# Final normalisation inside the expert steps, one ranked tile per pair of steps, and weight pieces issued as soon as their buffer is free

## What is computed

```python
def trunk_layer(...):                      # 2048 prompt rows and 32 sample rows, 1024 wide
    m = hybrid_mixer(x, ...)               # convolution mixer and recurrent block
    x = layer_norm(ALPHA * x + m, ln1_g, ln1_b)
    x = layer_norm(ALPHA * x + hier_moe(x, ...), ln2_g, ln2_b)

def hier_moe(x, ...):                      # top-1 group of 4, then top-2 experts of its 4
    ...
    h = silu(xt @ moe_w1[e]) * (xt @ moe_w3[e])
    h = h * gates
    y = sum over the token's two experts of h @ moe_w2[e]
```

## Time and profile before

| | |
|---|---|
| median of 3 runs | 1303.81 us (1301.26 to 1305.11) |
| profiled execution, its own time | 1298.67 us |
| its span | 1296.6 us |
| PE busy | 1140.4 us, 88% |
| DVE busy | 782.8 us, 60% |
| ACT busy | 503.3 us, 39% |
| POOL busy | 153.0 us, 12% |
| DMA read from and written to HBM | 133.99 MB, 72.93 MB |

### The profile page before, as it was taken

The page is one execution under the profiler, slowest core; times in us unless marked ns, Lnnn a source line. Parts: engine busy times, 40 slices in busy tenths (PEclk is TensorE's granted clock), DMA queues, the critical chain, the costliest instruction groups (busy, mean ns, idle before and its releaser), DMA issues. The chain is left out here.

```text
span 1296.6 us, 20522 instructions
## 1 busy us (share of the span) xinstructions
PE 1140.4 (88%) x5818; PEld 1028.6 (79%) x5819; DVE 782.8 (60%) x1476; ACT 503.3 (39%) x650; POOL 153.0 (12%) x192
## 2 busy tenths in 40 slices
PE   6999999999999999999999757999999999996000
PEld 6999999999999997888887655888888888875000
DVE  5666554644564565665665664566666666632898
ACT  4554443633543453222222224455555554421000
POOL 1000000000000010023322250000000000000720
PEclk9999999999999999999999877999999999998555
DMA  5432565275430055154433166667667776522972
GB/s 182 134 93 67 131 130 104 82 145 105 78 105 20 21 158 170 66 163 163 162 131 84 67 188 239 201 252 276 231 240 278 280 250 221 198 99 92 407 287 101
DMA packets 82772, 207.39 MB, mean 160 GB/s; under 512 B 18064, under 2 KB 44720, under 8 KB 76464
## 3 DMA queue, kind: packets, MB, share of 16 engines
q0 software_dynamic: 21984, 100.53, 21.7%
q1 hardware_dynamic: 53840, 89.63, 20.6%
q10 hardware_dynamic: 6912, 16.79, 7.5%
HBM read 133.99 MB, written 72.93 MB: 160 GB/s over the span
## 5 line engine op out<-in xcount | busy, mean ns | idle before, releaser
L1227 PE MATMUL ps_h<-w_hi,xt_hi 128*128 x336 | 136.4, 406 | 0.0
L1227 PE MATMUL ps_h<-w_lo,xt_hi 128*128 x336 | 132.4, 394 | 0.0
L1227 PE MATMUL ps_h<-w_hi,xt_lo 128*128 x336 | 132.3, 394 | 0.0
L277 PE MATMUL ps_vb_c<-x_hi,w_hi 128*128 (+1 forms) x320 | 113.9, 356 | 11.2 <-DVE x_lo L441 11.2
L277 PE MATMUL ps_vb_c<-x_hi,w_lo 128*128 (+1 forms) x320 | 113.3, 354 | 0.0
L277 PE MATMUL ps_va_b<-x_hi,w_lo 128*128 (+1 forms) x320 | 112.7, 352 | 0.0
L277 PE MATMUL ps_vb_c<-x_lo,w_hi 128*128 (+1 forms) x320 | 112.6, 352 | 0.0
L277 PE MATMUL ps_va_b<-x_hi,w_hi 128*128 (+1 forms) x320 | 112.6, 352 | 0.0
L277 PE MATMUL ps_va_b<-x_lo,w_hi 128*128 (+1 forms) x320 | 111.8, 349 | 0.0
L1321 DVE TENSOR_TENSOR w_lo_p<-ps_o,w_hi_p 128x512 f32<-128x512 f32 x84 | 54.0, 685 | 54.4 <-PE ps_o L1211 54.4
L1018 DVE TENSOR_TENSOR w_lo<-w_raw,w_hi 128x2048 f32 (+1 forms) x32 | 73.1, 2287 | 11.8 <-ACT w_hi L1013 11.8
(11 more groups left out here) (260 smaller groups left out, 2580.6 us busy)
## 6 DMA issues: line engine op xcount, KB each, us to landing
w_raw<-in_w POOLq DMA_DIRECT2D x48, 1024.0 KB, 6.0
w_lo_p<-xs_scr SPq DMA_DIRECT2D x43, 512.0 KB, 4.7
o_scr<-w_lo_p SPq DMA_DIRECT2D x42, 512.0 KB, 2.7
w_raw<-in_w_in POOLq DMA_DIRECT2D x19, 512.0 KB, 3.6
x_raw<-in_x_t SPq DMA_DIRECT2D x20, 416.0 KB, 3.4
xs_scr<-x_raw ACTq DMA_DIRECT2D x16, 512.0 KB, 7.0
o_scr<-x_raw ACTq DMA_DIRECT2D x16, 512.0 KB, 8.4
x_hi_p<-y_scr SPq DMA_DIRECT2D x16, 512.0 KB, 4.5
```

Of the source, the lines that this page charges most:

```text
L277: mm = pe.matmul(ps[i][:, 0:CHUNK], w[:, i, k], x[:, k, bass.ds(c * CHUNK, CHUNK)], start=(k == 0 and n == 0), stop=(k == KT - 1 and n == 2))
L1227: mm = pe.matmul(ps_h[par][:], x[:, par, k], w[:, bass.ds(at, 1), k].rearrange("p o n -> p (o n)"), start=(k == 0 and n == 0), stop=(k == ...
```

## The change

**Order of tiles.** The output tiles are no longer in token order. DVE ranks the tokens by the later of their two experts (`later_experts`, `ranks`, with two counting matmuls on PE), so that a tile of 128 consecutive ranks is complete as soon as that expert has been stored. Tile 0 has 32 tokens, tiles 1 to 16 have 128. Records (token number, two slots) go to DRAM by 17 indirect writes of POOL in step 0 and come back by one load. Results are written to `y_out` by indirect DMAs.

**Place of the work.** `steps` unrolls four steps, loops over pair numbers 2 to 15 with the body skipped from `pairs - FTAIL` on (FTAIL = 13), and then runs 13 pairs that carry output tiles: with 21 pairs the first gather is in step 17, tiles 0 to 9 are summed in the even steps 18, 20, ... 36 and normalised in the odd steps behind them, and steps 38 to 41 each sum a tile (10 to 13) and, from 39, normalise the one before. What is left of tiles 13 to 16 follows the last step. The number of pairs is raised if a tile would not be complete in time. `v` has two buffers, `v1` one: `fetch` of a tile waits until the tile ahead has been summed, until the tile two ahead has landed in `y_out`, and until the steps that it reads have been stored.

**ACT** takes the root in the steps, and in all but the last step runs a small Silu behind it. **Weights**: POOL takes them in the step where the raw buffers are freed (a flag in the plan), two experts ahead, without the waits for the landing of the piece ahead. **Zeros**: `fill` writes five blocks of `o_scr` each time, where it wrote two.

```diff
+FLAST = 2
+FPAIR = NT - 3 - 2 * FLAST
+FTAIL = FPAIR + FLAST + 1
+OFILL, STORED = 5, 8
+PLAN = 2 * ((STEPS - NT) // 2 + 1 + FTAIL)
...
-                for rows in (xs_scr[bass.ds((q * 2 + i) * CAP, P), :], o_scr[bass.ds((q * 2 + i) * P + (STEPS - NE) * P, P), :]):
-                    act.dma_start(rows, zero).then_inc(s_zo, 16)
+                act.dma_start(xs_scr[bass.ds((q * 2 + i) * CAP, P), :], zero).then_inc(s_zo, 16)
...
+            for i in range(OFILL):
+                act.dma_start(o_scr[bass.ds((q * OFILL + i + STORED) * P, P), :], zero).then_inc(s_zo, 16)
...
+            for s in range(4):
+                emit(s, s % 2, s // 2, 2, None)
+            eng.wait_ge(s_pairs, 1)
+            pairs = eng.value_load(planned[0:1, 0:1], min_val=0, max_val=PLAN // 2 - FTAIL - 2) + (FTAIL + 2)
+            with eng.Fori(2, PLAN // 2 - FTAIL) as h:
+                with eng.If(h < pairs - FTAIL):
+                    emit(h * 2, 0, h, 2, None)
+                    emit(h * 2 + 1, 1, h, 2, None)
...
+            def pair(f, b, h):
+                emit(h * 2, 0, h, 2, (None, (f, b), None))
+                emit(h * 2 + 1, 1, h, 2, ((f + 1, 1 - b), None, (f, b)))
+
+            h = pairs - FTAIL
+            emit(h * 2, 0, h, 2, None)
+            emit(h * 2 + 1, 1, h, 2, ((0, 0), None, None))
+            for f in range(2):
+                pair(f, f, pairs - (FTAIL - 1 - f))
+            with eng.Fori(0, (FPAIR - 2) // 2) as i:
+                for n in range(2):
+                    pair(i * 2 + (2 + n), n, i * 2 + (pairs - (FTAIL - 3 - n)))
+            tile = lambda f: (f, f % 2)
+            for n in range(2 * FLAST):
+                f = FPAIR + n
+                emit(pairs * 2 - (2 * FLAST - n), n % 2, pairs - (FLAST - n // 2), min(2, 2 * FLAST - 1 - n),
+                     (tile(f + 1), tile(f), tile(f - 1) if n else None))
...
-                pool.wait_ge(ew.s_r13[0], there)
                 load(e, 1)
...
-                pool.wait_ge(ew.s_r13[1], there)
                 load(e)
...
-            with pool.Fori(2, NE) as e:
-                weights(e)
+
+            def fetch(f, b, stored):
+
+                summed, free, copied = (count(pool, n) for n in (f, f * 16 - 16, f + 1))
+                if early(f, 1):
+                    pool.wait_ge(s_fin, 16)
+                else:
+                    pool.wait_ge(s_sum, 1)
+                    pool.wait_ge(s_sum, summed)
+                if not early(f, 2):
+                    pool.wait_ge(s_y, 16)
+                    pool.wait_ge(s_y, free)
+                pool.tensor_copy(id_f[:, b], fin[:, bass.ds(f, 1)].rearrange("p o n -> p (o n)")).then_inc(s_idf, 1)
...
+                for c, to in enumerate((v[b], v1)):
+                    pool.indirect_dma_start(to, None, o_scr[0:STEPS * P],
+                                            bass.IndirectOffsetOnAxis(id_f[:, b, 1 + c:2 + c], 0)).then_inc(s_v, 16)
+
+            def put(f, b):
...
+                pool.wait_ge(s_fn, 1)
+                pool.wait_ge(s_fn, done)
...
+                pool.indirect_dma_start(y_out, bass.IndirectOffsetOnAxis(id_f[0:n, b, 0:1], 0),
+                                        v[b][0:n], None).then_inc(s_y, 16)
...
+                more = pool.value_load(plan[0:1, 3, bass.ds(s, 1)], min_val=0, max_val=1)
+                with pool.If(more):
+                    weights(pool.value_load(plan[0:1, 0, bass.ds(s, 1)], min_val=0, max_val=NE - 3) + 2)
...
+            _, pair = steps(pool, step)
+            put(NT - 4, (NT - 4) % 2)
+            fetch(NT - 2, (NT - 2) % 2, (pair + 1, pair))
+            put(NT - 3, (NT - 3) % 2)
+            fetch(NT - 1, (NT - 1) % 2, (pair + 1, pair + 1))
+            put(NT - 2, (NT - 2) % 2)
+            put(NT - 1, (NT - 1) % 2)
+            pool.wait_ge(s_y, 16 * NT)
...
+                if tiles and tiles[1]:
+                    root(*tiles[1])
+                    if left:
+
+                        act.activation(idle[:], eps[:], ACT.Silu)
...
                 if left:
                     x_lo(s + 1, 1 - par)
+                if tiles:
+                    _, add, norm = tiles
+                    if norm:
+                        fin_norm(*norm)
+                    if add:
+                        fin_sum(*add)
                 with dve.If(split):
                     ew.lo13(dve, expert + 1, at, (0,))
...
             last, pair = steps(dve, step)
             h_lo(last)
+            fin_norm(NT - 4, (NT - 4) % 2)
+            fin_sum(NT - 3, (NT - 3) % 2)
             evict(last, 1, pair)
-
-
-def finish_phase(nc, o_scr, y_out, wreg, ln, sfin):
...
+            for f in (NT - 3, NT - 2):
+                fin_norm(f, f % 2)
+                fin_sum(f + 1, (f + 1) % 2)
+            fin_norm(NT - 1, (NT - 1) % 2)
```

280 lines of the change are left out of this document (177 added, 103 removed).

## The result

| | before | after |
|---|---|---|
| median (lowest to highest) | 1304.46 us (1301.26 to 1305.48) | 1326.49 us (1324.64 to 1332.64) |
| span of the profiled execution | 1296.6 us | 1324.9 us |
| PE, DVE, ACT, POOL busy | 1140.4, 782.8, 503.3, 153.0 us | 1177.4, 791.8, 539.4, 189.8 us |
| written to HBM | 72.93 MB | 85.53 MB |

The change makes the kernel slower: the ratio is 1.0181, with a 95% interval of 1.0144 to 1.0219. The forecast was 1262 us, 0.968. The two spans differ by 28.3 us and the medians by 22.0, because the profiled execution of before was 5.8 us under its median.

What follows compares the result with a forecast made beforehand. PE was taken to bound the expert steps, then idle for 104.2 us. 1296.6-1.5+1+7+14+3-65.3=1254.8 us span, 1256.9 with 2.07 outside, plus 5.1: 1262.0 us (0.968); forecast between 1245 and 1280, wider range 1238 to 1292.

Steps and rivals of the forecast that it cites:

- What bounds the kernel: Expert steps bound by PE, busy 389.1 of 394.3 us; the 104.2 us behind them leave PE idle and could be fed earlier.
- the number of steps: Expert steps: 21 pairs stay and no step is added, since the largest tile lateness is 2 pairs.
- step 16: Loop exit ahead of step 16: 8 skipped pairs cost 4.8 us plus 2.2 for the clock, +7 (bounds 4 and 9).
- Setup: Ahead of the steps: ranking fits DVE's idle time, expert 1's first weights come sooner, -1.5 us (bounds 0 and -4).
- Zeros: Three more DMAs in each of eight fills, mostly fitting ACT's gaps: +1 us (bounds 0 and +12).
- Tiles 0 to 9: Steps 18 to 37: DVE's summing and normalising makes hid late in eight split pairs, +14 us (bounds 5 and 44).
- Gathers in the steps: Gather lands at about 26 us after an even split step's start, DVE wants it at 25.7: +3 us (0 to 20).
- ACT: Two table loads of 1.28 us per tile, 3.1 us with the root, covered by some 2 us of slack: nothing.
- Late gathers: Rival: gathers in steps and tail land 6.3 us later, deciding from a landing of 10.1 us; +75, 1337 us, chance 0.07.
- The clock falls: Rival: late hid puts PE at the 1.2 GHz level after every split pair, 24 us more, 1286 us, chance 0.08.
- DVE becomes the bound: Rival: split pairs cost their whole 5.45 us or waits stand in each of ten; 1302 us, no change, chance 0.08.
- Tail: From step 37's transpose to the end: one tile per 11.1 us cycle, 85.5 us in place of 150.8, -65.3 us.

Runs made afterwards that it cites:

- run 1: Kernel before with only the zeros changed, five blocks of o_scr in each fill instead of two: 1303.22 us, ratio 1.0028 to before.
- run 6: Changed kernel with both gathers landing in buffers DVE does not read, so DVE waits for no gather (output wrong): 1273.59 us, 0.9788 of before.
- run 5: Changed kernel with stores waited for two pairs further back and the fetch moved to the even step ahead of the weights: 1283.49 us, 0.9846 of before.
- run 4: Changed kernel with the fetch of tiles 0 to 10 waiting for stores two pairs further back: 1299.67 us, ratio 1.0017 to before.
- run 14: Changed kernel with the fetch moved to the even step ahead of the weights, code of the store waits left alone: 1283.70 us, 0.9862 of before.

## Why the prediction was wrong, step by step

**What bounds the kernel, the number of steps, step 16** were right: 42 steps, the finish stage could be moved, and step 16 lost 7.6 us for a forecast of 7, by skips and the clock as stated.

**Setup.** -1.5 forecast, nothing measured. The gain is there: `hid` of step 0 is 2.9 us late for PE and no longer 4.0, and step 1 is 0.9 us shorter. But the first rows' load is issued at 791.3 where it was at 776.0, 3.3 us later than the mixer's shift accounts for. No term held the stall of step 2, 11.8 us. "The 17 index writes lie in POOL's idle time" looked at POOL's time only, not at what the burst may do to the others.

**Zeros.** I took +1 of bounds 0 to 12; 12.1 in this execution, 3.6 by run 1 in its mild session. The bound was about right, the value taken from it was not.

**Tiles 0 to 9.** 14 us for DVE's work; run 6 gives 16.7, so the size was about right, but the way was not quite the one forecast. `hid` should have been 1.0 and 1.2 us late for PE in each split pair. In run 5, PE waits for `hid` only 0.2 us in the whole stretch. It waits instead for 9.2 us, 16 times (twice in each of the eight split pairs), in front of the transposes that follow, for nothing that the profile shows. DVE and PE in step 20 of run 5:

```profile
1016.23 0.47 DVE L1483 SCALAR_TENSOR_TENSOR hid<-sil,gate,ps_h 128x256 f32<-128x256 f32 x1
```

```profile
1016.76 0.44 PE L1358 MATMUL ps_ht<-consts_sb,hid 128*128 128x128 f32 x2
1017.70 1.09 PE L1318 MATMUL ps_x<-consts_sb,w_lo_p 128*128 128x128 f32 x8 [0.51 <-issue]
```

`hid` is ready at 1016.70, just as PE's products end. Where it is ready earlier there is no such gap (up to step 15 none is over 0.2 us). I read this as PE's sequencer standing in the wait for `hid`, so that the register work of the next step, which it otherwise does ahead, is laid bare; this is argued from where the gaps lie and was not tried. The other 7.2 us are PE's own busy time (193.38 and 186.20). Some 3 us of them are its pace: its matmuls follow one another in 0.232 us where before 0.228 us did, in all kernels of this family (9.46 us for a step without tiles, not 9.31). That was not forecast; its cause, and what the last 4 us are, stays open.

**Gathers in the steps: this is the step that failed.** +3 was forecast, 33.6 measured. The working put the landing at about 26 us where DVE wants it at 25.7, a margin of nothing, on two rows of calm moments: the gather's 6.3 us, and no term for the store of step 2h-1, for which `fetch` waits by the diff. That store had a row, 2.7 us, but the sum put it at nothing without saying why. It lands in 6.8 us in the median once three weight pieces, two gathers and a result share the engines, and POOL stands up to 8.0 us for it. With that wait gone (run 4), 18.7 of the 33.6 us go; the rest goes when the fetch has more time to land (run 5). Whatever is late here is late three times: gather, `hid`, clock. Against run 5, PE has 21.8 us more of gaps and 12.0 us more of busy time in the stretch (31.2 and 9.4, 205.4 and 193.4), at a clock of 0.94 in place of 1.00.

**ACT** cost nothing that shows: `hid` waited for `sil` for 5.4 us in the stretch.

**The rivals.** "Late gathers" was the true one, at a chance of 0.07, and it came at a landing of 7.3 us, far under the 10.1 from which I let it decide: I had counted the landing alone and not the wait ahead of the issue. "The clock falls" came as its consequence. "DVE becomes the bound" did not.

**Tail.** -65.3 forecast; from `hid` of step 37 to the end 95.4 us, where before took 152.8: -57.4. The cycle was forecast at 11.1 us and is 11.5 in the mean (9.1 to 12.9); the last gather landed 5.4 us after its issue. The term that was mis-sized is the last write, "1.0+about 3.5" for 13.0 us. For the gather the figure of the Trainium skill ("DMA: Bandwidth & Descriptors", section "Anatomy of one DMA — SWDGE (gpsimd) path"), an estimated 3.2 us, is again lower than the trace: 5.4 us for the last gather, which had its twin and, from 3.3 us on, one result's write beside it.

Together: 11.1 (zeros), 1.4 (setup), 11.8 (step 2), 3.8 (steps 3 to 15, of which 1.6 in step 3, right behind the stall), 0.7 (steps 16 and 17), 33.4 (steps 18 to 37) and 7.9 (tail) are, to the rounding, the 70.1 us (1324.9-1254.8) between the forecast span and the measured one.

## What to carry to other kernels

When work is moved into a stage that is bound elsewhere, let the request for its data wait for nothing that is fresh, and put it where it has a whole period to land, ahead of the bulk transfers in its queue: here the first was worth 18.7 us and the second 15.1 us more, without touching the work. Take the landing time of a transfer from the load that it will meet, and count the waits in front of its issue with it. A sum in which the data land just when they are wanted (here at about 26 us for 25.7) has no room for a term left out. And when an edit moves a piece of code, look at which branch its conditions take in the new place: run 14 dropped a wait that it was meant to keep.
